# A fused two-block transformer kernel: which expert rows TensorE adds up, and when the second memory is fetched and normed

## The chip, the cores and the metric

One core of one Trainium2 chip runs the whole program. The metric is the device time in microseconds of one execution; lower is better. TensorE is called PE here (PEld is its weight load), VectorE DVE, ScalarE ACT, GpSimd POOL and SyncE SP.

## What is computed

The reference is two transformer blocks over 512 tokens of width 1024, all in fp32. The first block has a mixer (a gated short convolution and causal differential attention), cross-attention to a memory of 256 rows, and then the part that the change is about, a lookup of single-neuron experts:

```python
q = (hc @ w_pq).reshape(PEER_CHUNK, PEER_HEADS, 2, PEER_DK_HALF)
sc = jnp.einsum('thcd,chnd->thcn', q, sub_keys)
vals, idx = lax.top_k(sc, PEER_TOPK)              # per head and key half: 16 of 128
... # the 16x16 sums of both halves, top 16 of them -> experts, gates g (softmax)
ue = peer_u[experts]; ve = peer_v[experts]        # 16384 experts, rows of 1024
act = jax.nn.gelu(jnp.einsum('td,thkd->thk', hc, ue), approximate=False)
y = jnp.einsum('thk,thkd->td', g * act, ve)
```

Each token uses 8 heads x 16 = 128 experts. The second block has sparse attention, a gMLP and a convolution branch, cross-attention to a second memory (`mem_2`, normed with its own gain, then projected to keys and values), and a feed-forward of width 2816 with a short convolution.

## The kernel before

**Halves and tiles.** The tokens are 4 tiles of 128, and two tiles make a half. Half 0 goes through the first block's mixer and cross-attention alone. Then three streams run side by side until about 2390 us: `work` (the mixer of half 1, its cross-attention, its expert scores, the second memory, and the whole second block of half 0), `peers` (the experts of tiles 0 to 3) and `choices` (top-k selection of tiles 0 to 3). After that the second block of half 1 runs alone.

**What sets the order.** The class `Plan` is a host-side generator. `weave` gives each of the three streams a clock, always takes a step from the stream whose clock is lowest, and adds the number that the step carries. The result is one list of steps, and each engine executes, in that order, those of its instructions that belong to each step. All queues are in order, so an instruction that waits holds all behind it on its engine. Semaphores do the rest.

**One expert.** An expert number k = 128 t + c is column c of tile t: one of 128 experts for each of the tile's 128 tokens. POOL gathers its rows (U and V side by side, 128 x 2048 fp32, 1 MB) with an indirect DMA into one of 8 slots (L2073). DVE takes the dot product with the tokens (L1856, and writes over the U half). ACT applies the gelu (L1357) and multiplies by the gate (L1361, or L1364). Then the V row is added, in one of two ways:

- DVE: `scalar_tensor_tensor` into the residual tile X (L1836), one expert later in the order.
- PE: ACT first writes a diagonal matrix of the gates (L1369, tile DG or a piece of BIG), and PE multiplies it with the V row's two halves into PSUM banks 6 and 7 (L1092, L1093), placed two experts later in the order. At a tile's end DVE adds the two banks to X (L1846).

The slot is free for the gather of k+8 once the sum is done, so POOL waits for L1836 or L1093. `pe_sums` lists the experts that PE sums. Before, an expert is put there while `light` is set (in half 1's attention, cross-attention and expert scores, the second memory, and half 0's sparse attention), two of three.

**Choices.** `choose` finds the experts of one tile in 4 parts p of 2 heads each, on DVE: L1764, L1767 and L1772 (top 8 values, their places, and their removal), L1779, L1798, L1801, L1804, then L1811 writes the indices. Tiles 0 and 1 are chosen while tile 0's experts run (k = 0 to 74); that ends with part (1, 3). `work` may not load the weights of k (half 1's attention keys) before it, and their eviction to SBUF waits for it too.

**Projections.** Weights come in entries of 512 KB through a ring of 6 (SP queue, L698). A `proj_T` entry is 8 matmuls of 128x256 (L833 seven times, L834), a `proj_tok` entry L853 and L854. Each result takes one of 6 PSUM banks in turn while experts run. Sites are named by their weights: cc, cx, cb (convolution; DVE multiplies, L1565, L1570, L1582), cv, gc (DVE, L1587), q, k, v, then the attention `da`.

**Norms.** `norm_steps` is a norm's squares on ACT (L1139), mean and reciprocal on DVE (L1509, L1511), the root on ACT (L1144), and the product with the inverse root for both tiles, tile 1 on DVE (L1521), tile 0 on ACT (L1161) or, where `norm_of` says `pool=True`, on POOL (L2042). `trans` follows: 16 PE transposes (L821, L822) and the evictions with the gain (L1170 on ACT).

**The second memory.** `memory(2, True)` comes after all four quarters of the scores of half 1: ACT issues the load of `mem_2` (1 MB, L1129), waits, norms it, PE transposes it and projects it (sites nk, nv).

## Time and profile before

| | us |
|---|---|
| median of 3 runs | 3008.01 (3006.35 to 3032.95) |
| the profiled execution | 3006.38 |
| its span in the trace | 3004.7 |
| PE busy, share of the span | 2483.7 (83%) |
| DVE busy | 1812.6 (60%) |
| ACT busy | 1117.7 (37%) |
| mean granted PE clock | 0.887 |
| experts' gathers | 512, from 559.4 to 2364.6 us, 536.90 MB |

The span is what the profiler saw from the first to the last instruction; the execution's own time has 1.7 us around it, and the median of the runs is 1.6 us above the profiled one. Busy shares are means over stretches with different limits, so they say little by themselves: the three streams run from 559 to 2390 us, and within that each stretch has its own busiest engine. An expert's time is read by its dot product: k = 0 at 565.9 us, 74 at about 879, 93 at 926.5, 151 at 1101.4, 215 at 1331.0, 255 at 1524.8 and 511 at 2384.2.

### The profile page before, as it was taken

How to read it: one execution, taken by the hardware profiler on the slowest of the kernel's cores; microseconds unless marked ns; L12 is line 12 of the kernel's file. 1: busy time of each engine (PE TensorE's matmuls, PEld its weight loads, DVE VectorE, ACT ScalarE, POOL GpSimd, SP SyncE). 2: the span in 40 equal slices, each digit the busy share in tenths (PEclk: the TensorE clock that was granted, in tenths of full speed). 3: DMA queues.
4: the chain of work that ended last, by engine and by line, in shares of the span. 5: the costliest groups of instructions: out<-in, count | busy, mean ns of one | idle time of the engine just before them, and what ended most of it. 6: DMA issues, size and time to landing. Idle time of an engine off the chain costs nothing.

```text
span 3004.7 us, 29173 instructions
## 1 busy us (share of the span) xinstructions
PE 2483.7 (83%) x9938; PEld 1784.8 (59%) x9938; DVE 1812.6 (60%) x4267; ACT 1117.7 (37%) x2717; POOL 696.8 (23%) x568
## 2 busy tenths in 40 slices
PE   8999998776957779789768888588988399788998
PEld 7786765665843446547536744365863177655883
DVE  2101312699998678668779997778997705512430
ACT  1101312231525663543342576564552213512210
POOL 0000000122345344332223535344323301100100
PEclk9999999888978889899889578799999695799999
DMA  6545243779999999998689998899999740032443
GB/s 198 170 153 167 92 160 108 290 295 343 387 409 420 350 383 415 419 378 318 257 307 400 419 341 338 323 409 416 417 417 418 320 135 29 1 106 82 151 152 119
DMA packets 156644, 827.08 MB, mean 275 GB/s; under 512 B 16920, under 2 KB 20392, under 8 KB 90704
## 3 DMA queue, kind: packets, MB, share of 16 engines
q0 software_dynamic: 73728, 536.90, 44.7%
q1 hardware_dynamic: 78144, 276.21, 26.2%
q10 hardware_dynamic: 4624, 12.11, 1.1%
q8 instruction: 79, 1.29, 0.2%
q14 instruction: 69, 0.57, 0.1%
HBM read 816.74 MB, written 8.41 MB: 275 GB/s over the span
## 4 chain that ended last, share of the span: by engine, by line
PE 50%; DVE 22%; ACT 14%; DMA 9%; issue 4%; POOL 1%; ACTq 0%; DVEq 0%; SPq 0%
PE ps L833 21%; DVE X L1836 6%; DMA BIG<-in_uv,BIG 6%; DVE BIG L1856 6%; PE ps L853 5%; PE ps L854 5%; PE ps L834 3%; PE ps L1070 3%; ACT L1357 2%; PE ps L974 2%; DVE BIG L1767 1%; PE ps L1092 1%; ACT WK L1139 1%; PE ps L1093 1%; DMA BIG<-head_scratch 1%
## 5 line engine op out<-in xcount | busy, mean ns | idle before, releaser
L2073 POOL DMA_INDIRECT BIG<-in_uv,BIG x512 | 647.3, 1264 | 1706.9 <-DVE X L1836 693.9
L833 PE MATMUL ps<-BIG,RING 128*128 128x256 f32 x3472 | 812.6, 387 | 75.0 <-ACT BIG L1190 31.6
L833 PEld LDWEIGHTS ps<-BIG,RING 128*128 128x128 f32 x3472 | 671.6, 194 | 186.0 <-ACT BIG L1190 32.0
L1856 DVE CUSTOM_DVE_ANT_0 BIG<-BIG 128x1024 f32<-128x1024 f32 x512 | 620.2, 1217 | 54.2 <-DMA BIG<-in_uv,BIG 53.3
L1836 DVE SCALAR_TENSOR_TENSOR X<-BIG,small,X 128x1024 f32<-128x1024 f32 x378 | 484.2, 1281 | 86.6 <-ACT small L1361 86.4
L1357 ACT ACTIVATE small<-small 128x1 f32<-128x1 f32 x512 | 102.7, 201 | 703.6 <-DVE small L1856 702.0
L833 PE MATMUL ps<-WK,RING 128*128 128x256 f32 x1232 | 290.2, 388 | 16.1 <-DVE BIG L1615 14.2
L833 PEld LDWEIGHTS ps<-WK,RING 128*128 128x128 f32 x1232 | 238.0, 194 | 56.7 <-DVE BIG L1615 21.2
L853 PE MATMUL ps<-RING,BIG 128*128 128x512 f32 (+1 forms) x448 | 224.1, 582 | 7.1 <-DVE BIG L1594 4.4
L854 PE MATMUL ps<-RING,BIG 128*128 128x512 f32 (+1 forms) x448 | 223.5, 580 | 0.0
L1190 ACT ACTIVATE BIG<-ps 128x256 f32<-128x256 f32 (+2 forms) x143 | 56.3, 396 | 381.5 <-PE ps L834 322.8
L821 PE MATMUL ps<-ident,BIG 128*128 128x128 f32 x128 | 50.9, 404 | 150.0 <-ACT BIG L1161 83.1
L1553 DVE TENSOR_SCALAR BIG<-ps 128x256 f32<-128x256 f32 (+2 forms) x37 | 16.8, 454 | 255.8 <-PE ps L834 211.3
L1070 PE MATMUL ps<-RING,BIG 128*128 128x512 f32 x352 | 156.7, 607 | 8.9 <-DVE BIG L1615 8.9
L1357 ACT ACT_TABLE_LOAD x121 | 155.2, 1283 | 2.8 <-issue 0.6
L834 PE MATMUL ps<-BIG,RING 128*128 128x256 f32 x496 | 147.5, 379 | 0.0
L853 PEld LDWEIGHTS ps<-RING,BIG 128*128 128x128 f32 x448 | 84.9, 191 | 104.7 <-issue 92.2
L854 PEld LDWEIGHTS ps<-RING,BIG 128*128 128x128 f32 x448 | 85.4, 191 | 101.5 <-issue 100.1
L1546 DVE TENSOR_TENSOR X<-ps,X 128x512 f32<-128x512 f32 x40 | 27.3, 690 | 196.1 <-PE ps L854 124.8
L1139 ACT ACTIVATE WK<-X 128x1024 f32<-128x1024 f32 x32 | 33.8, 1056 | 258.2 <-DVE X L1546 242.7
L1070 PEld LDWEIGHTS ps<-RING,BIG 128*128 128x128 f32 x352 | 67.9, 194 | 96.8 <-issue 84.0
L821 PEld LDWEIGHTS ps<-ident,BIG 128*128 128x128 f32 x128 | 27.3, 213 | 159.4 <-ACT BIG L1161 88.0
(257 smaller groups left out, 3261.2 us busy)
## 6 DMA issues: line engine op xcount, KB each, us to landing
RING<-in_w_up SPq DMA_DIRECT2D x88, 512.0 KB, 6.1
RING<-in_w_down SPq DMA_DIRECT2D x44, 512.0 KB, 6.1
RING<-in_w_pq SPq DMA_DIRECT2D x32, 512.0 KB, 4.3
RING<-in_w_cc SPq DMA_DIRECT2D x16, 512.0 KB, 7.9
RING<-in_w_cx SPq DMA_DIRECT2D x16, 512.0 KB, 4.8
RING<-in_w_cb SPq DMA_DIRECT2D x16, 512.0 KB, 5.3
RING<-in_w_cv SPq DMA_DIRECT2D x16, 512.0 KB, 4.5
RING<-in_w_gc SPq DMA_DIRECT2D x16, 512.0 KB, 6.5
```

Source lines behind the costliest of these rows:

```text
L821: e.transpose(ps[:, 0:128], tmp[:, 0, k * 128:(k + 1) * 128], ident[:, :])
L833: e.matmul(ps[:, 0:256], W[:, j, :], src[:, j, 0:256], start=j == 0, stop=False)
L834: e.matmul(ps[:, 0:256], W[:, 7, :], src[:, 7, 0:256], start=False, stop=True).then_inc(pe.sem, pe("mm", site, h, c, m))
L853: e.matmul(ps[:, 0:n], src[:, 2 * j, t * 128:(t + 1) * 128], W[:, 0, :], start=j == 0, stop=False)
L854: mm = e.matmul(ps[:, 0:n], src[:, 2 * j + 1, t * 128:(t + 1) * 128], W[:, 1, :], start=False, stop=j == 3)
L974: mm = e.matmul(ps[pr, 0:nn], W1[l // 16][:, l % 16, :], KN[pr, s, f0:f0 + 16 * nn - 15:16], start=l == 0, stop=l == 31)
L1070: mm = e.matmul(ps[:, :], AF[:, f, t * 128:(t + 1) * 128], W[:, hh * 512:(hh + 1) * 512], start=f == 0, stop=f == 21)
L1139: e.activation(SQ[:, 0:width], src(i), ACT.Square, accum_out=small[:, o + i:o + i + 1]).then_inc(act.sem, act("sq", key, i))
L1357: e.activation(a, dots[:, k % 8:k % 8 + 1], ACT.Gelu).then_inc(act.sem, act("gelu", k))
L1836: e.scalar_tensor_tensor(out=X[:, t, :], in0=slot[slot_of[k]][:, 1024:2048], scalar=acts[:, k % 8:k % 8 + 1], in1=X[:, t, :], op0=ALU.mult ...
L1856: e.tensor_tensor_reduce(out=u, in0=HF[:, t % 2, :], in1=u, scale=1.0, scalar=0.0, op0=ALU.mult, op1=ALU.add, accum_out=dots[:, k % 8:k % ...
L2073: e.indirect_dma_start(out=slot[i], out_offset=None, in_=I["uv"], in_offset=bass.IndirectOffsetOnAxis(ap=IDX[:, t, c:c + 1], axis=0)).then ...
```

## The change

Four things change.

1. While part (1, 3) isn't chosen yet, an expert goes to PE every second time, although `light` is not set. These are 37 of the experts 0 to 74, which all were DVE's before.
2. A flag `norming` is set from a lean norm's start to the end of its transposes, and for the last two steps of half 1's and of half 0's attention units before one; while it is set, no expert goes to PE. Together with the shifted count this gives, by the plan, 59, 48, 37 and 17 experts on PE in tiles 0 to 3 (161), where it was 23, 54, 41 and 16 (134).
3. The load of `mem_2` is issued at the start of half 1's expert norm. Its norm comes after the second quarter of half 1's scores, the transposes after the fourth. For that its tile lies at W0 + 6144, where the values of the first block's cross-attention lay, which are dead by then.
4. The two norms of half 1's second block that used POOL for tile 0 use ACT.

```diff
@@ norm_steps, norm, da
     def norm_steps(self, key, lean):
         gap = 2.6 if lean else 0
+        self.norming = lean
         yield gap, "norm_sq", key
...
         for k in range(8):
             yield (cost if k == 7 else 0), "trans", key, k, lean
+        self.norming = False
...
-        yield from self.phase(True, (((5.0 if h == 0 else 9.0), "da", h, i) for i in range(20)))
+        for step in self.phase(True, (((5.0 if h == 0 else 9.0), "da", h, i) for i in range(20))):
+            self.norming = h == 1 and step[3] >= 18
+            yield step
@@ memory
-    def memory(self, tag, lean):
-        yield 0, "mark", ("mem", tag)
-        yield 0, "mem_in", tag
-        yield from self.norm(("mem", tag), lean)
-        yield from self.proj_T("mk" if tag == 1 else "nk", tag, 2, lean)
-        yield from self.proj_tok("mv" if tag == 1 else "nv", tag, 2, lean)
+    def memory(self):
+        yield from self.proj_T("nk", 2, 2, True)
+        yield from self.proj_tok("nv", 2, 2, True)
@@ experts
         yield 0, "mark", ("ffn", h)
+        if h == 1:
+            yield 0, "mem_in", 2
         yield from self.norm(("ffn", h), lean)
@@ scores
             for t in range(2):
                 yield 0.9, "scores", h, c, t, lean
+            if h == 1 and c == 1:
+                yield 0, "mark", ("mem", 2)
+                yield from self.norm_steps(("mem", 2), lean)
+                self.norming = False
+            if h == 1 and c == 3:
+                for i in range(8):
+                    yield 0, "trans", ("mem", 2), i, lean
@@ second (the 20 steps of the sparse attention; set back after the transposes of y)
-        yield from self.phase(True, ((8.0, "nsa", h, i) for i in range(20)))
+        for step in self.phase(True, ((8.0, "nsa", h, i) for i in range(20))):
+            self.norming = lean and step[3] >= 18
+            yield step
@@ peers
-                if self.light:
+                if not self.norming and (self.light or (1, 3) not in self.chosen):
                     n += 1
-                    if n % 3:
+                    if n % 3 if self.light else n % 2:
                         self.pe_sums[t].append(k)
@@ program, norm_of
-               2: dict(M=at_(W0 + 8192, 2, 1024), MT=at_(W0 + 10240, 8, 256), TMP=at_(W0 + 8192, 2, 1024),
+               2: dict(M=at_(W0 + 6144, 2, 1024), MT=at_(W0 + 10240, 8, 256), TMP=at_(W0 + 6144, 2, 1024),
...
-                return dict(src=half(h), g="mix2", dst=HTz, tmp=TMPz, o=0, pool=h == 1)
+                return dict(src=half(h), g="mix2", dst=HTz, tmp=TMPz, o=0, pool=False)
...
-                return dict(src=half(h), g="ffn2", dst=HTu, tmp=at_(L0, 2, 1024), o=0, pool=h == 1)
+                return dict(src=half(h), g="ffn2", dst=HTu, tmp=at_(L0, 2, 1024), o=0, pool=False)
```

The new lines shift the line numbers of the changed kernel by up to 15: L1092 and L1093 are L1107 and L1108 there, L833 is L848, L1139 is L1154, and so on.

How PE's queue changes while tiles 0 and 1 are chosen: the start of half 1's projections, at site cc, after the norm's transposes. The banks are ps0 to ps7. Before:

```order
L833 MATMUL ps5<-BIG,RING 128x256 x7
L834 MATMUL ps5<-BIG,RING 128x256
L833 MATMUL ps0<-BIG,RING 128x256 x7
L834 MATMUL ps0<-BIG,RING 128x256
L833 MATMUL ps1<-BIG,RING 128x256 x7
L834 MATMUL ps1<-BIG,RING 128x256
L833 MATMUL ps2<-BIG,RING 128x256 x7
L834 MATMUL ps2<-BIG,RING 128x256
```

The same place now:

```order
L848 MATMUL ps5<-BIG,RING 128x256 x7
L849 MATMUL ps5<-BIG,RING 128x256
L848 MATMUL ps0<-BIG,RING 128x256 x7
L849 MATMUL ps0<-BIG,RING 128x256
L1107 MATMUL ps6<-BIG,DG 128x512
L1108 MATMUL ps7<-BIG,DG 128x512
L848 MATMUL ps1<-BIG,RING 128x256 x7
L849 MATMUL ps1<-BIG,RING 128x256
L848 MATMUL ps2<-BIG,RING 128x256 x7
L849 MATMUL ps2<-BIG,RING 128x256
```

Between every second pair of weight entries stands a sum, two matmuls of 128x512 that need an expert's diagonal.

ACT's queue where the second memory is normed. Before, at the end of half 1's scores, right before PE's transposes of it (L1345 evicts the last scores):

```order
L1369 ACTIVATE BIG<-ident,small 128x128
L1129 DMA BIG<-in_mem_2 128x2x1024
L1139 ACTIVATE WK,small<-BIG 128x1024 x2
L1351 ACT_TABLE_LOAD
L1351 ACTIVATE BIG<-BIG 128x32
L1144 ACT_TABLE_LOAD
L1144 ACTIVATE small<-small 128x2
L1357 ACT_TABLE_LOAD
L1357 ACTIVATE small<-small 128x1
L1361 ACTIVATE small<-small,BIG 128x1
L1161 ACTIVATE BIG<-BIG,small 128x1024
```

Now, in the middle of the scores, with the load issued 62 rows earlier, ahead of the squares of the expert norm:

```order
L1384 ACTIVATE BIG<-ident,small 128x128
L1154 ACTIVATE WK,small<-BIG 128x1024 x2
L1372 ACTIVATE small<-small 128x1
L1376 ACTIVATE small<-small,BIG 128x1
L1159 ACT_TABLE_LOAD
L1159 ACTIVATE small<-small 128x2
L1176 ACTIVATE BIG<-BIG,small 128x1024
L1372 ACT_TABLE_LOAD
```

The load no longer stands right ahead of the squares that need it. The evictions of the third quarter (L1205) now stand behind the norm in this queue.

PE's queue at the end of half 1's attention, from the last of the 16 transposes (ps4) into the projection ga. Before:

```order
L821 MATMUL ps4<-ident,BIG 128x128
L822 MATMUL ps4<-ident,BIG 128x128
L833 MATMUL ps5<-BIG,RING 128x256 x7
L834 MATMUL ps5<-BIG,RING 128x256
L1092 MATMUL ps6<-BIG 128x512
L1093 MATMUL ps7<-BIG 128x512
L833 MATMUL ps0<-BIG,RING 128x256 x7
```

The sum there is expert 151's, and POOL's gather for its slot waits for it. Now:

```order
L836 MATMUL ps4<-ident,BIG 128x128
L837 MATMUL ps4<-ident,BIG 128x128
L848 MATMUL ps5<-BIG,RING 128x256 x7
L849 MATMUL ps5<-BIG,RING 128x256
L848 MATMUL ps0<-BIG,RING 128x256 x7
L849 MATMUL ps0<-BIG,RING 128x256
```

The sum behind the first entry of ga is gone, and so are the last ones ahead of the transposes: the experts 145, 146, 148, 149 and 151 are DVE's.

## Rows read from the trace of the kernel before

**Rows 1.** The page's groups: line, engine, operation, count, busy us, mean ns

```profile
L1856 DVE CUSTOM_DVE_ANT_0 BIG<-BIG 128x1024 f32<-128x1024 f32 x512 | 620.2, 1217 | 54.2 <-DMA BIG<-in_uv,BIG 53.3
...
L1836 DVE SCALAR_TENSOR_TENSOR X<-BIG,small,X 128x1024 f32<-128x1024 f32 x378 | 484.2, 1281 | 86.6 <-ACT small L1361 86.4
```

**Rows 2.** Waits, whole span: us in total, times, longest us

```profile
POOL BIG L2073 <- DVE X L1836: 693.9, 303, 9.6
...
POOL BIG L2073 <- PE ps L1093: 418.1, 99, 28.8
```

**Rows 3.** Windows: busy PE, PEld, DVE, ACT, POOL, PEclk, DMA share, GB/s

```profile
565.90:870.00 304.10, 227.37 (x1017) 197.19 (x1015) 284.25 (x707) 100.83 (x244) 79.87 (x73) 0.88 0.93 361
...
722.00:752.00 30.00, 7.99 (x35) 6.40 (x35) 29.93 (x78) 3.98 (x16) 8.13 (x9) 0.72 0.92 345
...
786.00:848.00 62.00, 62.00 (x289) 54.59 (x288) 56.14 (x128) 34.62 (x65) 17.46 (x15) 1.00 1.02 417
...
848.00:882.00 34.00, 9.26 (x43) 7.80 (x42) 33.73 (x67) 6.14 (x21) 13.00 (x11) 0.70 1.02 419
...
882.00:930.00 48.00, 36.22 (x96) 19.29 (x96) 46.16 (x61) 15.19 (x53) 30.57 (x20) 0.89 1.00 406
```

**Rows 4.** Waits of PE from 566 to 930 us

```profile
PE ps L833 <- ACT BIG L1190: 31.6, 1, 31.6
...
PE ps L833 <- DVE BIG L1582: 22.0, 2, 21.1
...
PE ps L821 <- DVE BIG L1521: 17.7, 1, 17.7
...
PE ps L950 <- ACT BIG L1190: 16.7, 2, 14.4
```

**Rows 5.** Chain of waits, 1433 to 1536 us: start, us, what

```profile
1433.23 10.63 DMA BIG<-in_mem
...
1456.61 3.26 PE ps L833 x14
...
1460.30 0.86 PE ps L1092 x2
...
1461.16 0.86 PE ps L1093 x2
...
1535.12 0.87 PE ps L1093 x2
```

**Rows 6.** Line L1369: count, min/median/max ns

```profile
L1369 ACT ACTIVATE DG<-ident,small x68: 401/402/403, 930.8 to 2384.9; 128x128 f32<-128x128 f32 x68
```

**Rows 7.** Timeline of PE at 751 us: start, us, instruction, count

```profile
751.32 5.36 PE L833 MATMUL ps<-BIG,RING 128*128 128x256 f32 x14 [21.12 <-DVE BIG L1582]
...
756.95 3.19 PE L833 MATMUL ps<-BIG,RING 128*128 128x256 f32 x14
```

**Rows 8.** Waits of PE and of DVE from 1336 to 1545 us

```profile
PE ps L821 <- ACT BIG L1161: 29.3, 2, 20.8
...
DVE small L1509 <- ACT WK L1139: 13.4, 1, 13.4
```

**Rows 9.** Windows around the second memory's norm

```profile
1384.00:1432.00 48.00, 44.89 (x188) 33.96 (x186) 43.74 (x149) 16.39 (x43) 11.54 (x12) 0.96 0.85 308
...
1432.00:1453.00 21.00, 0.80 (x4) 0.80 (x5) 7.45 (x35) 9.09 (x16) 1.45 (x1) 0.57 0.45 171
```

**Rows 10.** Waits of POOL from 1095 to 1130 us

```profile
POOL BIG L2073 <- PE ps L1093: 19.4, 3, 17.1
```

**Rows 11.** Windows at two norms, at 1113 and at 1900 us

```profile
1113.00:1125.00 12.00, 12.00 (x50) 10.07 (x49) 11.90 (x20) 5.72 (x10) 2.17 (x3) 0.82 0.56 203
...
1900.00:1912.00 12.00, 2.67 (x13) 2.71 (x14) 6.70 (x17) 8.09 (x24) 1.15 (x2) 0.50 0.26 87
```

**Rows 12.** Timeline: POOL at half 1's last norm; an ACT copy alike

```profile
2758.20 3.40 POOL L2042 TENSOR_SCALAR BIG<-X,small 128x1024 f32<-128x1024 f32 x1 [157.96 <-ACT small L1144]
...
1451.02 1.13 ACT L1161 ACTIVATE BIG<-BIG,small 128x1024 f32<-128x1024 f32 x1
```

More of the change, by code:

```diff
@@ L232, in mixer @@
             yield (3.0 if k == 7 else 0), "trans", ("o", h), k, lean
+        self.norming = False
         yield from self.proj_T("ga", h, 2, lean)
@@ L280, in scores @@
                 yield 0.9, "scores", h, c, t, lean
+            if h == 1 and c == 1:
+                yield 0, "mark", ("mem", 2)
+                yield from self.norm_steps(("mem", 2), lean)
+                self.norming = False
+            if h == 1 and c == 3:
+                for i in range(8):
+                    yield 0, "trans", ("mem", 2), i, lean
             self.reached.add(("sc", h, c))
@@ L330, in second @@
             yield (2.0 if k == 7 else 0), "trans", ("y", h), k, lean
+        self.norming = False
         yield from self.proj_tok("ou", h, 2, lean)
@@ L368, in work @@
             yield step
-        for step in self.memory(2, True):
+        for step in self.memory():
             self.light = True
@@ L1287, in mem_in @@
                     for q in ENGINES:
-                        w.wait_ge(*at["mark", ("mem", tag), q])
+                        w.wait_ge(*at["mark", ("ffn", 1), q])
                 load(f"mem{tag}", m["M"], I[m["src"]].rearrange("a (t p) d -> p (a t) d", p=128), "mem", tag)
```

## The prediction

> **What bounds the kernel now.** I read the page's groups first, to see what an expert costs and who adds it: the dot product takes 1217 ns of DVE, and 378 of 512 sums are DVE's at 1281 ns [rows 1]. So a DVE sum doubles an expert's price there. Then the waits, to see who holds the slots: POOL waited 693.9 us for DVE's sums and 418.1 us for PE's [rows 2], 2.3 us a sum (303) against 4.2 us (99). Then the windows, stretch by stretch, because each has its own limit.
>
> While tiles 0 and 1 are chosen (565.9 to about 880 us, experts 0 to 74), DVE is busy 284.25 of the first 304.1 us, the DMA moves 361 GB/s where saturated stretches show 417 to 419, and PE is busy 227.37 us [rows 3]. DVE is the fullest. But within the stretch the limits change places: from 722 to 752 us DVE has 29.93 of 30 us and PE 7.99; from 786 to 848 us PE is busy all 62 us and the DMA is full; from 848 to 882 us DVE has 33.73 of 34 us and PE 9.26 [rows 3]. PE's four longest waits there are 31.6 us (the eviction of the keys, held until part (1, 3) is chosen), 21.1 of 22.0 us (cb waits for DVE's L1582), 17.7 us (the norm) and 14.4 of 16.7 us [rows 4]; this is the room for sums on PE.
>
> From 1336 us, after half 1's expert norm, the chain of waits runs through PE: from 1456.61 to the last sum of tile 1, which starts at 1535.12, entries and sums follow each other without a hole. The one large hole ahead of them is the second memory's norm, which begins with its load, 10.63 us [rows 5]. PE waits 20.8 us for ACT's product with the root there, DVE 13.4 us for the squares [rows 8], and from 1432 to 1453 us PE is busy 0.80 us and the DMA runs at 0.45 [rows 9].
>
> **Part 1, every second sum on PE until (1, 3) is chosen.** 37 sums leave DVE: 37 x 1.281 = 47.4 us less of 284.25 plus what runs to 880 us. They come to PE, and one is two pieces of 0.86 us in an unbroken chain [rows 5], 1.72 us: 37 x 1.72 = 63.6 us more. ACT writes 37 diagonals of 402 ns [rows 6], 14.9 us on an engine that is busy 100.83 of 304.1 us [rows 3]; nothing for that, since its idle time hides it (15 us at most if that cover were gone).
>
> Upper bounds of the gain: the DMA must move 361 x 304.1 GB/s x us, at 417 that is 263 us, so 41 us at most; DVE, 47 us at most. The tighter one is PE. Over 565.9 to 930 us (with the keys' and values' entries behind the choices) it is busy about 227 + 4 + 36 = 267 us, the 4 being its share of 870 to 882 us. With the sums it has 331 us of 364. Some idle time must stay: the norm's own chain, waits for the first multiplications, the start behind the choices; I take 10 to 35 us. That gives 341 to 366 us, a gain of 23 to -2 us.
>
> The pieces in order: the norm ends earlier by the five sums that DVE no longer makes ahead of it, 6 us. PE then reaches cb later by ten sums, 17 us, which mostly uses up the 21.1 us wait, while DVE comes there some 19 us earlier; start of cb some 8 to 10 us earlier. From 752 to 848 us PE has no idle time, and 12 more sums cost it 21 us, so it ends q about 12 us later than now; but behind q it waits 31.6 us today, so this is covered. DVE's choices, ten experts further, need 33.73 us now and five sums less, 27 us, and can run up to the slots' depth ahead of PE; (1, 3) would be chosen some 15 us earlier. What is late next are PE's entries for keys and values: today five of them already stand in PSUM when (1, 3) comes, and now sums of experts up to 72 stand ahead of them in PE's queue, so perhaps two do. Three entries of some 3.5 us each (14 of their 16 passes take 3.19 to 3.26 us) [rows 5, 7], 10 us, are then missing, and the DMA is full from 882 to 930 us as well (406 GB/s) [rows 3]. I take 12 us, the middle of the bound from PE's sum, with both ends kept (23 and -2), and -10 as the end where chances of order fall badly.
>
> Of the clock, the trace shows that the first 14 matmuls after the 21.1 us wait took 5.36 us and the next 14 took 3.19 [rows 7], which is 1.2 against 2.4 GHz for part of them; the mean granted clock is 0.72 in that window and 1.00 from 786 us. The Trainium skill (TensorE: Matmul & The Clock Gate, "Why this matters for your kernels") says to leave no idle gaps between bursts, because the clock drops after them. By that rule sums that fill the gaps pay back some 2 us at each of three gaps, and the gain would be 18 instead of 12 us; the trace agrees that there is a loss behind a gap, but the gaps become shorter rather than disappear.
>
> **Part 2, the memory.** The load goes out about 110 us before it is needed, at a time when ACT waits for all engines anyway (the marks of the expert norm), so its wait of 10.63 us goes. The norm's steps then run while PE works on the scores. The wait of PE, 20.8 us, goes whole, since only the 16 transposes stay. Is something else late in its place? DVE is busy 43.74 of 48 us from 1384 to 1432 us [rows 9], but only 7.45 of the next 21 us, so its choice work fits if it flows over. The norm now stands in ACT's queue ahead of evictions of pq, and ACT waits for DVE's reciprocal; PE runs up to six banks ahead, 20 us, so I charge 1 to 5 us and take 3. The plan puts two sums less on PE in this stretch (27 for 29), 3 us less; the last two parts of tile 3's choices slip by one or two experts into DVE's full stretch behind, about 1 us. Sum 20.8 - 3 + 3 - 1 = 20 us, range 12 to 24. Floor: nothing if PE's hole just moves.
>
> **Part 3, no sums beside a norm.** At the end of half 1's attention POOL waits 17.1 us for one PE sum that stands behind 16 transposes and an entry [rows 10], and the DMA falls to 203 GB/s for 12 us; before the second block's norm in half 0 it falls to 87 GB/s for 12 us [rows 11]. With DVE as the adder, slots free earlier: of these holes of 6 and 9.5 us I count 4 us in all, since the DVE chain that causes the norm itself stays, and DVE gets up to two sums, 2.6 us, ahead of each norm. Range -4 to 10. Tiles 1 and 2 have 10 sums more on DVE, 13 us in stretches where DVE isn't full: nothing.
>
> **Part 4, POOL to ACT.** Twice POOL takes 3.40 us for a product on which the transposes wait, where ACT takes 1.13 us for such a copy [rows 12]: 2 x 2.27 = 4.5 us off a chain with nothing beside it. The Trainium skill (GPSIMD Engine Reference, "4.1 Engine selection") calls one-input elementwise work on GpSimd "roughly line-rate", by which the move would bring next to nothing and the sum below would be 4.5 us smaller; the row disagrees, and the measured 3.40 us decides.
>
> **The sum.** 12 + 20 + 4 + 4.5 = 40.5 us off the span of 3004.7 is 2964; with the 1.7 us around the span and the 1.6 us between the profiled execution and the median it is 2968 us, 1.3% faster. Without a change of kernel, a measurement here can tell about 1% apart.
>
> **Rivals.**
> - *PE takes over as the bound while tiles 0 and 1 are chosen.* For it: PE is at 100% for 62 us at a stretch [rows 3], and each sum adds 1.72 us there. Against it: the 31.6 us wait behind. Part 1 then gives -5 instead of 12: 2985 us.
> - *The relief goes through whole.* PE's idle time shrinks to 10 us, and the DMA holes at the norms close: part 1 gives 23, part 3 gives 10: 2951 us. Against it: the DMA is saturated from 786 us on.
> - *The memory's norm only moves its hole.* If ACT, waiting for DVE's reciprocal, holds the evictions past the six banks, PE stands still in the scores. Part 2 gives 5: 2983 us.
> - *Slower.* PE's queue holds the slots. A PE sum kept POOL waiting 4.2 us against 2.3 us for DVE's [rows 2]; if that reaches the gathers, 37 x 1.9 = 70 us are lost, with nothing of the 47 us gained, and 3008 + 70 - 28.5 (parts 2 to 4) = 3050 us. It decides once DVE's dot products wait for gathers over the whole stretch; today that wait is 53.3 us over the whole program [rows 1].
>
> That the change doesn't do what it says is no rival: the instruction order shows it.
>
> **Chances.** Forecast 0.46 (own range 2955 to 2981), PE as bound 0.23, relief whole 0.14, the hole moved 0.10, slower 0.07. Faster by over 1% means below 2978: most of the forecast (0.39), the whole relief (0.14) and some of the two that lie between (0.08), 0.61. Slower by over 1% is 0.06, the rest, 0.33, is within 1%. The range from 2944 to 3001 leaves out the slower rival and the tails of the others.
>
> **What would show it.** Right: 161 PE sums; experts 0 to 74 in about 300 us instead of 313, with DVE near 80% and PE near 90% in it; no PE wait of 20 us near 1440, and tile 1's last sum about 32 us earlier than 1535; DMA above 300 GB/s in the 12 us behind half 1's attention norm; no POOL product in the last 600 us. Wrong: DVE waiting for gathers from 600 to 850 us, PE waiting for L1369's diagonals (then the sums come too early in its queue), or a new PE wait of over 10 us within the scores. The largest unknown is how much of DVE's 47 us survives PE's 64.

## The result, and the profile after

The changed kernel takes 2983.74 us (median of 18 runs, 2974.98 to 3003.74) against 3007.79 us before in the same measurement (18 runs, 3003.32 to 3038.33): a ratio of 0.9904 with an interval of 0.9876 to 0.9931, 1.0% faster. The ratio takes in all runs; that of the two medians is 0.9920, since six of the 18 runs before took 3027 us or more. The forecast was 2968 us and 1.3%. The profiled execution has a span of 2990.2 us and a mean granted clock of 0.897, against 3004.7 us and 0.887. It took 2992.0 us, 8.3 us more than the median, so that the trace shows less of the gain than the runs do.

The page's groups for the dot products and DVE's sums, of after:

```profile
L1871 DVE CUSTOM_DVE_ANT_0 BIG<-BIG 128x1024 f32<-128x1024 f32 x512 | 618.9, 1219 | 64.6 <-DMA BIG<-in_uv,BIG 63.1
L1851 DVE SCALAR_TENSOR_TENSOR X<-BIG,small,X 128x1024 f32<-128x1024 f32 x351 | 450.3, 1283 | 103.7 <-ACT small L1376 103.5
```

351 sums are DVE's where 378 were [rows 1], so PE has 161. The lines quoted here have numbers 15 higher than before (L1856 is now L1871). In two windows, the choices of tiles 0 and 1 (dots 0 to 74) and the stretch to dot 93, with PE, PEld, DVE, ACT and POOL busy, clock, DMA share and GB/s:

```profile
563.80:864.20 300.40, 265.62 (x1067) 202.77 (x1067) 250.85 (x685) 115.52 (x284) 88.86 (x75) 0.95 0.95 362
864.20:921.60 57.40, 57.40 (x196) 37.79 (x195) 45.33 (x64) 16.93 (x54) 24.25 (x19) 0.98 1.02 418
```

The first took 313.1 us and takes 300.4; PE is now 88% busy in it and DVE 84%. The second took 47.5 us and takes 57.4, and PE has not one idle moment in it; before it was busy 36.22 of about 48 us [rows 3]. Of 12.7 us won, 9.9 are given back. PE's waits in the first window show what the sums filled; 31.6 and 21.1 us were the longest before [rows 4]:

```profile
PE ps L836 <- DVE BIG L1536: 13.3, 1, 13.3
PE ps L965 <- ACT BIG L1205: 8.8, 1, 8.8
PE ps L1107 <- ACT DG L1384: 6.0, 3, 3.3
PE ps L1107 <- ACT BIG L1384: 5.6, 3, 4.0
```

At the second memory PE's waits from 1330 to 1540 us are now these, where 20.8 us stood for the norm [rows 8]:

```profile
PE ps L836 <- ACT BIG L1176: 8.4, 1, 8.4
PE ps L965 <- ACT BIG L1205: 8.0, 2, 7.4
PE ps L1107 <- ACT BIG L1384: 6.2, 1, 6.2
PE ps L848 <- ACT BIG L1185: 2.9, 2, 1.9
PE ps L1107 <- ACT DG L1384: 2.3, 1, 2.3
PE ps L836 <- ACT BIG L1185: 1.3, 1, 1.3
```

The 8.4 us are the expert norm's own, which was there before. The scores' longest wait for an eviction is 7.4 us; it was 2.5 us. Behind half 1's attention POOL waits (1085 to 1125 us) for DVE's sum where it waited 17.1 us for PE's [rows 10], and at the second block's norm (1876 us) the DMA is as empty as it was [rows 11]:

```profile
POOL BIG L2088 <- DVE X L1851: 20.8, 10, 13.7
POOL BIG L2088 <- PE ps L1108: 1.0, 1, 1.0
```

```profile
1876.00:1888.00 12.00, 3.27 (x16) 3.06 (x16) 6.42 (x17) 8.13 (x24) 2.17 (x2) 0.54 0.26 87
```

In half 1's norms ACT and DVE make a tile each at the same time, 1.15 us, instead of 3.40 us on POOL [rows 12]:

```profile
2373.61 1.15 ACT L1176 ACTIVATE WK<-X,small 128x1024 f32<-128x1024 f32 x1
2373.61 0.75 DVE L1536 TENSOR_SCALAR WK<-X,small 128x1024 f32<-128x1024 f32 x1 [0.27 <-ACT small L1159]
```

Set against the first dot of each trace, the gain is then 12.7 us at dot 74, 2.8 at 93, 2.7 at 213, 16.9 at the mix2 norm's transposes in half 0 (1002.0 and 985.1 us behind the first dot), 22.0 at dot 363 and 24.0 at the last. Behind that 11.5 us are lost. The place is half 1's sparse attention, from the end of the compression's matmuls to the first transpose of the y norm: 136.2 us before, 154.7 now. I call it **the late stretch**. Windows of 30 us in it, before and after; PEclk is the column ahead of the DMA share:

```profile
2484.00:2514.00 30.00, 27.44 (x167) 23.02 (x166) 15.32 (x76) 11.10 (x29) 3.84 (x3) 0.50 0.18 69
2514.00:2544.00 30.00, 30.00 (x103) 23.73 (x102) 19.36 (x96) 14.43 (x48) 5.12 (x4) 0.50 0.00 1
2544.00:2574.00 30.00, 30.00 (x99) 21.88 (x99) 16.10 (x77) 11.77 (x33) 6.08 (x4) 0.54 0.00 1
2574.00:2604.00 30.00, 30.00 (x208) 24.87 (x206) 21.82 (x107) 21.28 (x55) 8.00 (x5) 1.00 0.01 2
```

```profile
2458.00:2488.00 30.00, 26.59 (x134) 21.00 (x133) 19.57 (x97) 14.34 (x40) 5.12 (x4) 0.56 0.11 36
2488.00:2518.00 30.00, 30.00 (x105) 23.99 (x104) 16.63 (x85) 12.17 (x40) 5.12 (x4) 0.50 0.00 1
2518.00:2548.00 30.00, 30.00 (x95) 21.64 (x94) 16.51 (x77) 12.19 (x33) 4.79 (x3) 0.50 0.00 1
2548.00:2578.00 30.00, 30.00 (x101) 22.74 (x100) 14.15 (x68) 11.16 (x31) 4.79 (x3) 0.50 0.00 1
2578.00:2608.00 30.00, 22.33 (x147) 19.95 (x145) 14.58 (x64) 13.09 (x32) 3.20 (x2) 0.78 0.00 1
```

The work is the same. PE does it at 1.2 GHz (0.50), about 100 matmuls in 30 us, until the clock is granted in full, then 208. The next lines narrow down its return, to some 2571 us of the span before and to 2580 us now:

```profile
2566.00:2574.00 8.00, 8.00 (x32) 6.00 (x31) 5.10 (x23) 3.73 (x10) 1.60 (x1) 0.66 0.00 0
```

```profile
2575.00:2583.00 8.00, 8.00 (x35) 6.14 (x34) 4.19 (x21) 3.73 (x10) 1.60 (x1) 0.69 0.00 0
```

The stretch begins at 2495.3 and at 2464.6 us, so the clock is back 76 us into it before and 115 us into it now. These 39 us more of PE's work at half the clock are worth about half as much, and the stretch is 18.5 us longer.

### The profile page after: what moved, and what is told of

It reads as the page before. It is cut to its first block, busy times and chain, and to the rows that moved or that the text cites. A ratio compares the mean times of both kernels' runs of the same rounds, so it can differ in the third digit from the quotient of the medians.

```text
span 2990.2 us, 29389 instructions
## 1 busy us (share of the span) xinstructions
PE 2533.2 (85%) x10046; PEld 1804.9 (60%) x10046; DVE 1781.5 (60%) x4240; ACT 1130.7 (38%) x2747; POOL 706.2 (24%) x566
## 4 chain that ended last, share of the span: by engine, by line
PE 56%; DVE 18%; ACT 12%; DMA 9%; issue 4%; POOL 1%; ACTq 0%; DVEq 0%; SPq 0%
PE ps L848 25%; DMA BIG<-in_uv,BIG 7%; PE ps L868 6%; PE ps L869 5%; DVE BIG L1871 5%; DVE X L1851 4%; PE ps L849 3%; PE ps L1085 3%; ACT L1372 2%; PE ps L989 2%; PE ps L1107 2%; PE ps L1108 2%; PE ps L1057 2%; DMA BIG<-head_scratch 1%; PE ps L1036 1%
## 5 line engine op out<-in xcount | busy, mean ns | idle before, releaser
L2088 POOL DMA_INDIRECT BIG<-in_uv,BIG x512 | 663.6, 1296 | 1664.5 <-DVE X L1851 575.4
L848 PE MATMUL ps<-BIG,RING 128*128 128x256 f32 x3472 | 804.1, 384 | 15.9 <-DMA RING<-in_w_cq 4.8
L848 PEld LDWEIGHTS ps<-BIG,RING 128*128 128x128 f32 x3472 | 667.7, 193 | 134.5 <-issue 26.7
L1871 DVE CUSTOM_DVE_ANT_0 BIG<-BIG 128x1024 f32<-128x1024 f32 x512 | 618.9, 1219 | 64.6 <-DMA BIG<-in_uv,BIG 63.1
L1851 DVE SCALAR_TENSOR_TENSOR X<-BIG,small,X 128x1024 f32<-128x1024 f32 x351 | 450.3, 1283 | 103.7 <-ACT small L1376 103.5
L848 PE MATMUL ps<-WK,RING 128*128 128x256 f32 x1232 | 287.3, 385 | 18.7 <-DVE BIG L1630 16.7
L848 PEld LDWEIGHTS ps<-WK,RING 128*128 128x128 f32 x1232 | 235.9, 193 | 58.8 <-DVE BIG L1630 23.9
L1205 ACT ACTIVATE BIG<-ps 128x256 f32<-128x256 f32 (+2 forms) x143 | 56.4, 397 | 398.0 <-PE ps L849 338.3
L1107 PE MATMUL ps<-BIG,DG 128*128 128x512 f32 x162 | 97.2, 685 | 56.8 <-ACT DG L1384 56.7
L1154 ACT ACTIVATE WK<-X 128x1024 f32<-128x1024 f32 x32 | 33.8, 1056 | 257.5 <-DVE X L1561 243.4
```

The source lines that it names most:

```text
L848: e.matmul(ps[:, 0:256], W[:, j, :], src[:, j, 0:256], start=j == 0, stop=False)
L1107: e.matmul(banks[6][:, :], d, v[:, 0:512], start=first, stop=last)
L1851: e.scalar_tensor_tensor(out=X[:, t, :], in0=slot[slot_of[k]][:, 1024:2048], scalar=acts[:, k % 8:k % 8 + 1], in1=X[:, t, :], op0=ALU.mult ...
L1871: e.tensor_tensor_reduce(out=u, in0=HF[:, t % 2, :], in1=u, scale=1.0, scalar=0.0, op0=ALU.mult, op1=ALU.add, accum_out=dots[:, k % 8:k % ...
L2088: e.indirect_dma_start(out=slot[i], out_offset=None, in_=I["uv"], in_offset=bass.IndirectOffsetOnAxis(ap=IDX[:, t, c:c + 1], axis=0)).then ...
```

## Experiments

Three theories were open at the start: that part 1's gain is lost at the keys' and values' entries; that the memory's norm, ahead of the evictions in ACT's queue, makes the new 7.4 us wait; and that part 4, which alone touches what lies directly ahead of the late stretch, keeps its clock low. Against each stands that the difference is the scatter between executions. Twelve kernels were run, the changed one again among them. Each ratio is against runs of the kernel before made together with it. Their medians were 3011.3 us for the four single parts, 3016.7 for pool_norms, mix2_pool, early_keys and split_norm, 3009.9 for the extra matmuls and all_sums, and 3006.6 for the changed kernel again, so medians of different measurements don't rank kernels by themselves.

**One part at a time.** Each is the kernel before with one part of the change:

```diff
 # sums_only: part 1, without the norming flag
+                if self.light or (1, 3) not in self.chosen:
+                    if n % 3 if self.light else n % 2:
 # memory_only: part 2 (mem_in in experts, norm_steps and transposes in scores, the new addresses)
 # norms_only: part 3, on the old sums
+                if self.light and not self.norming:
 # act_norms_only: part 4
-    mix2, ffn2: pool=h == 1
+    mix2, ffn2: pool=False
```

> The kernel before with part 1 alone (every second sum on PE until (1, 3) is chosen). Theory A (PE takes the gain back right behind the choices): experts 0 to 74 take some 300 us instead of 313, experts 74 to 93 some 57 instead of 47.5 us, so 3 us are left at expert 93; PE has an unbroken run of about 58 us through the keys' and values' entries. Theory B (the loss there comes from something else in the full change): experts 74 to 93 stay at 48 us and 12 us are left at expert 93. Total, by A: within 6 us of before; by B 12 us faster.

> The kernel before with part 2 alone (memory loaded at the expert norm, normed among the scores). Theory A (a new wait inside the scores eats a third): PE waits some 7 us for an eviction of pq that stands behind the norm in ACT's queue, and the stretch from the expert norm's transposes to those of the second block's norm (499.8 us from 502.2 before) becomes 13 to 14 us shorter. Theory B (the smaller gain comes from the sums that were shifted): no such wait, 20 us shorter.

> The kernel before with part 3 alone (no sum on PE beside a norm). Theory A (it is worth next to nothing, since the DVE chain of the norm sets the time): total within 4 us of before, POOL's 17.1 us wait at 1105 us gone. Theory B: slots that come free earlier fill the DMA hole, 4 to 8 us faster, and most of it behind half 1's attention and half 0's sparse attention.

> The kernel before with part 4 alone (two products from POOL to ACT). Everything up to the last expert is the same program, so up to there nothing moves. Behind it: 2.3 us less at each of the two norms, 4.5 us in all. What the sparse attention of half 1 between them takes (136 us before, 155 us in the changed kernel, with PE's granted clock at half for longer) tells the theories apart on that loss: if it is caused by part 4 it shows here too in the profile and in the times (about 14 us slower); if it is a matter of chance of the clock, it takes 136 us here or 155 us, whatever the kernel.

| kernel | median us (runs) | ratio, interval | profiled span | late stretch | span less its excess over 136.2 |
|---|---|---|---|---|---|
| before | | | 3004.7 | 136.2 | 3004.7 |
| changed | 2983.7 (18) | 0.9904, 0.9876 to 0.9931 | 2990.2 | 154.7 | 2971.7 |
| sums_only | 3020.5 (10) | 1.0018, 0.9988 to 1.0048 | 3020.9 | 162.4 | 2994.7 |
| memory_only | 3003.6 (10) | 0.9966, 0.9925 to 1.0006 | 3005.8 | 150.1 | 2991.9 |
| norms_only | 2999.3 (10) | 0.9947, 0.9912 to 0.9982 | 3031.0 | 168.2 | 2999.0 |
| act_norms_only | 3024.0 (10) | 1.0027, 0.9999 to 1.0055 | 3016.1 | 154.7 | 2997.6 |

By their ratios the four parts bring -0.2, 0.3, 0.5 and -0.3%, 0.4% together, while the whole brings 1.0%. The last column seems to agree better: 10.0, 12.8, 5.7 and 7.1 us, 35.6 together, and 33.0 for the whole. How good this is depends on scatter: a second execution of the changed kernel (below) gives 25.5, and all four differences lean on the one trace before. That the late stretch spoils the sum of the ratios is likely by this, not shown. Part 4 alone makes the two norms shorter and yet measured no faster.

Part 1 alone, its two windows:

```profile
564.00:867.40 303.40, 267.90 (x1069) 203.61 (x1068) 249.77 (x684) 115.80 (x285) 85.89 (x75) 0.94 0.93 359
867.40:924.30 56.90, 56.90 (x195) 37.53 (x194) 45.24 (x64) 16.90 (x54) 25.52 (x19) 0.98 1.02 419
```

9.7 us are won to dot 74 and 9.4 given back by dot 93 (360.2 us in all, 360.6 before). Part 2 alone: from the expert norm's to the mix2 norm's transposes 218.7 us instead of 231.9, 13.2 us less. Part 3 alone: the POOL wait at 1100 us is DVE's, 13.6 us, and row 213 comes 2.6 us earlier.

**The control on scatter.** The program of act_norms_only is the kernel before's up to the last row, and still its dot 151 came 4.0 us later and dot 303 3.4 us. Then the changed kernel was run again:

> The changed kernel itself, unedited, on the chip of this call. Theory E (the moment at which TensorE's clock returns in half 1's sparse attention differs between executions, and its spread is the spread of the times): up to the last row's dot this execution agrees with the first one within 5 us (1789 to 1799 us behind the first dot), the stretch from the compression's end to the y transposes is again anywhere from 136 to 168 us, the profiled span less what the stretch takes above 136.2 us is 2967 to 2977 us, and the runs lie between 2972 and 3010 us. Rival F (the moment is a property of the kernel, and the edits of the other experiments moved it): the stretch is 150 to 158 us again, and the median 2980 to 2988 us.

2985.1 us (12 runs, 2978.7 to 3013.0), ratio 0.9917 (0.9881 to 0.9954). The two executions agree within 1.3 us up to dot 363, 1855 us into the span, and differ by 6.8 us at the last dot. Four more traces below are of the same program up to the last dot; all six lie within 1.5 us of each other at dots 93 and 120, but spread over 6 us at dots 213 and 363 and over 7.7 us at the last. So behind dot 120 a single trace tells an effect below some 6 to 8 us from scatter only where it shows the wait. The late stretch took 154.8 us, against 154.7; rival F's number, where theory E left 136 to 168 open, and the median is in F's range as well. The span less the excess is 2979.2, above the 2967 to 2977 that E wanted. These two profiles don't show the scatter of the runs to be the late stretch's.

**Part 4 undone in the changed kernel**, for both norms and for mix2 alone:

```diff
-            if kind == "mix2":  ... pool=False)
+            if kind == "mix2":  ... pool=h == 1)
-            if kind == "ffn2":  ... pool=False)     # pool_norms only
+            if kind == "ffn2":  ... pool=h == 1)    # pool_norms only
```

> The changed kernel with part 4 undone: GpSimd again makes the squares and the scaling of the norms before half 1's two last expert layers. The two norms themselves should take their 4.5 us back (last dot to the mix2 transposes 18.8 instead of 16.7 us, x(2,1) to ffn2's transposes 91 instead of 88.8). Theory A: ACT's norm is what keeps TensorE at 1.2 GHz longer in half 1's sparse attention (154.7 us from the end of the compression to the y transposes instead of 136.2). Then this stretch is 136 to 142 us again and the time is 2965 to 2975 us, ratio 0.985 to 0.989. Rival B: when the clock returns there is chance or hangs on everything before it. Then the stretch is anything between 136 and 168 us, and the median is that of the changed kernel plus 4.5 us, 2986 to 2990 us, ratio 0.991 to 0.993.

> The changed kernel with part 4 undone for the mix2 norm alone, the one ahead of the stretch at 1.2 GHz; ffn2's norm, behind the stretch, stays on ACT. Theory A (ACT's mix2 norm keeps the clock low longer): stretch 136 to 142 us, time 2962 to 2973 us, ratio 0.984 to 0.988, and 2.3 us below the kernel with both norms on GpSimd. Rival B (chance): 2985 to 2988 us, ratio 0.991 to 0.993.

Only the products move; the squares are ACT's in every kernel, though the expectation gives them to GpSimd. Medians 3009.7 us (12 runs, ratio 0.9947, 0.9914 to 0.9980) and 3006.5 us (12, 0.9947, 0.9914 to 0.9981). The late stretch took 162.4 and 150.0 us. Theory A falls: with POOL back in its place the stretch is not short again. Both are above rival B's medians too. The spans less the excess are 2978.4 and 2978.0 us.

**More work for PE in the late stretch.** If the clock's return hung on how much PE does there, extra matmuls would bring it earlier. The score matmuls are issued twice, into the same PSUM:

```diff
+                        if h and j == 0 and u < 8:    # more_cols_32: if h and j < 2
+                            e.matmul(ps[:, 0:nn], q, K, start=True, stop=True)
                         e.matmul(ps[:, 0:nn], q, K, start=True, stop=True).then_inc(...)
```

> The changed kernel, with the first score matmul of the first 8 of 16 units of half 1's sparse attention issued twice (same operands, same PSUM, the second overwrites the first), in the stretch that runs at 1.2 GHz: 8 matmuls of 384 columns, some 7 us more if the clock stays low. Theory C (how much TensorE has to do in this stretch decides when its clock returns, and the changed kernel is near the edge): the clock is back at 185 us behind the last dot or sooner, the stretch from the compression's end to the y transposes is 120 to 142 us in place of 154.7, and the runs lie close together, 2968 to 2985 us. Rival D (TensorE's load there does not matter to it): the stretch is 143 to 175 us as by chance, and the median is 2988 to 2993 us.

> As the kernel with 8 matmuls doubled, but with both large score matmuls of all 16 units of half 1's sparse attention issued twice: 32 more, of 384 and 512 columns, some 30 us more at 1.2 GHz and 15 at 2.4. Theory C: the clock is back in the first 60 us of the stretch, which then takes 110 to 135 us, and the time is 2955 to 2980 us. Rival D (the load does not matter): the stretch is 165 to 200 us, and the median 3005 to 3015 us.

3006.1 us (10 runs, 2982.8 to 3017.7; ratio 0.9980, 0.9952 to 1.0009), stretch 144.0 us; and 3032.8 us (10, 3011.5 to 3057.2; 3025.2 without the longest, which the ratio leaves out; 1.0089, 1.0053 to 1.0126), stretch 173.2 us. The first stretch alone could be read either way (theory C wanted 120 to 142, rival D 143 to 175), but its runs are scattered over 35 us. The clock is back 84 us into it with 8 more matmuls and 105 us with 32, where the changed kernel has 115 us and the kernel before 76. Both lie within what kernels without extra work show, the larger load has the later return, and neither is near the first 60 us, where theory C had it for 32. In that form theory C falls; a small effect of the load within this scatter isn't excluded. Less its excess, extra matmuls included, the spans are 2976.3 and 2972.8 us: the same program everywhere else.

**The keys ahead again.** No PE sum from row 63 on while tile 1 is chosen:

```diff
-                if not self.norming and (self.light or (1, 3) not in self.chosen):
+                if not self.norming and (self.light or ((1, 3) not in self.chosen and k < 63)):
```

> The changed kernel, but with no sum on TensorE from row 63 on while tile 1 is chosen, so that key and value entries can run ahead again (row 74 then comes about 3 us later than in the changed kernel). Theory (TensorE had 58 us of unbroken work there, 864 to 922 us, and its key entries came late): the dot of row 93, counted from the first dot, comes 9 to 12 us before that of the kernel before instead of 2.8, and the time is 4 to 8 us below the changed kernel's 2984, ratio 0.988. Rival (the gain is lost to whatever comes next, since DVE has its sums back): row 93 moves by less than 3 us, 2984 us, ratio 0.9905.

```profile
563.00:868.20 305.20, 273.15 (x1141) 215.62 (x1139) 256.65 (x689) 113.84 (x281) 88.66 (x75) 0.96 0.94 362
868.20:920.80 52.60, 36.73 (x96) 19.64 (x96) 46.37 (x64) 15.38 (x51) 28.39 (x19) 0.86 1.01 420
```

The entries do run ahead: PE has 15.9 us free in the second window. But DVE, with its sums back, is 4.7 us later at dot 74, and dot 93 comes at 357.7 us behind the first, against 357.8 in the changed kernel: the rival's reading, for this step. What the second window shows is a full DMA, 420 GB/s; it is 418 in the changed kernel's, 419 in sums_only's and 406 from 882 to 930 us before [rows 3]. The gathers of rows 74 to 93 are at the DMA's limit either way. Dot 120 came 6.3 us earlier than in the changed kernel, where the traces of that program differ by 1.5 us at most, so this is real; but by dot 151 it was 2.3 us later, and the gain was gone. The time was 2979.2 us (6 runs, 2974.5 to 2984.0), ratio 0.9872 (0.9835 to 0.9908), the lowest of all, but its late stretch took 136.2 us, and less the excess its span of 2978.8 us is not below the changed kernel's 2971.7 and 2979.2. Its intervals overlap with the changed kernel's as well. It isn't shown to be better.

**The memory's norm in two pieces**, root and product a quarter later:

```diff
             if h == 1 and c == 1:
-                yield from self.norm_steps(("mem", 2), lean)
+                yield 0, "norm_sq", ("mem", 2); yield 0, "norm_inv", ("mem", 2)
+            if h == 1 and c == 2:
+                yield 0, "norm_root", ("mem", 2); yield 0, "norm_out", ("mem", 2)
```

> The changed kernel with the second memory's norm in two pieces: squares and their sum after the second quarter of the key scores, root and scaling after the third. Theory (the scores' evictions wait behind the whole norm in ACT's queue, 7.4 us at 1409.6): TensorE's longest wait of its score matmuls on an eviction falls below 4 us, the stretch from ffn(1)'s to mix2(0)'s transposes shrinks from 217.8 to about 213 us, and the time is 3 to 5 us lower, 2980 us, ratio 0.989. Rival (the second piece makes its own wait, and the memory's transposes come later): the two add up to the same 217 to 219 us, 2984 us, ratio 0.9905.

Its waits of PE from 1380 to 1460 us:

```profile
PE ps L968 <- ACT BIG L1208: 8.2, 2, 7.3
PE ps L839 <- ACT BIG L1188: 4.1, 1, 4.1
```

The wait of the scores for the eviction is 7.3 us as before, and a wait of the memory's transposes for their evictions comes in addition; from transposes to transposes the stretch takes 222.7 us against 217.8. The time was 3010.4 us (12 runs, ratio 0.9967, 0.9940 to 0.9995), its late stretch 168.2 us.

Going by the wait alone would clear the norm, but the wait misleads. The starts of the second and the third quarter's scores, first in the kernel before and then in split_norm, are

```profile
1380.12 1.95 PE L950 MATMUL ps<-WK,BIG 128*128 128x128 f32 x16
1403.53 3.23 PE L950 MATMUL ps<-WK,BIG 128*128 128x128 f32 x16 [2.49 <-ACT BIG L1190]
```

```profile
1374.45 1.95 PE L968 MATMUL ps<-WK,BIG 128*128 128x128 f32 x16
1402.68 3.75 PE L968 MATMUL ps<-WK,BIG 128*128 128x128 f32 x16 [7.32 <-ACT BIG L1208]
```

That is 23.4 us before and 28.2 with the norm's first piece alone in this quarter. With the whole norm, in the changed kernel, it is 34.3 us (34.0 in memory_only, 22.6 in sums_only and norms_only, which don't have it). So the norm in this place costs some 11 us; PE has one sum more there than before, which its 7.4 us wait covers. Its second piece moved away gives 6.1 of them back, and 1.7 us are lost in the next quarter and 9.2 from the last scores to the transposes behind. The first eviction of the third quarter shows it: it starts 7.7 us after the second scores before (1387.77), 12.6 in split_norm and 14.4 in the changed kernel. What follows it, PE and ACT around the wait in the changed kernel, is

```profile
1373.49 1.95 PE L965 MATMUL ps<-WK,BIG 128*128 128x128 f32 x16
1399.32 1.02 PE L1108 MATMUL ps<-BIG,DG 128*128 128x512 f32 x2
1407.78 3.75 PE L965 MATMUL ps<-WK,BIG 128*128 128x128 f32 x16 [7.44 <-ACT BIG L1205]
```

```profile
1400.61 0.20 ACT L1372 ACTIVATE small<-small 128x1 f32<-128x1 f32 x1 [4.78 <-DVE small L1871]
1400.84 0.29 ACT L1379 ACTIVATE small<-small,BIG 128x1 f32<-128x1 f32 x1
1401.17 0.40 ACT L1384 ACTIVATE BIG<-ident,small 128x128 f32<-128x128 f32 x1
1401.48 0.36 ACT L1205 ACTIVATE BIG<-ps 128x256 f32<-128x256 f32 x1
1406.84 0.20 ACT L1372 ACTIVATE small<-small 128x1 f32<-128x1 f32 x1 [5.00 <-DVE small L1871]
1407.07 0.29 ACT L1376 ACTIVATE small<-small,BIG 128x1 f32<-128x1 f32 x1
1407.27 0.36 ACT L1205 ACTIVATE BIG<-ps 128x256 f32<-128x256 f32 x1
```

In ACT's queue one row's activation and one eviction take turns. The activation waits 4.78 and 5.00 us for its dot product, since DVE, busy 23.01 of 24 us from 1386 to 1410, works on tile 2's choices between two dots. The eviction behind it was ready, and PE waited for it. The kernel before has the same turns, with waits of 4.45 and 5.29 us, but its evictions had begun earlier and took 15.3 us from the first to the fourth, where they take 19.4 now. So 6.8 of the 11 us are the norm's delay of the first eviction, and the rest are longer turns behind it.

**All sums of that phase on PE**, the rival in which it becomes the bound:

```diff
-                    if n % 3 if self.light else n % 2:
+                    if n % 3 if self.light else True:
```

> The changed kernel, but every V row's sum is TensorE's while tiles 0 and 1 are chosen, 37 or so more than in the changed kernel. Theory (TensorE becomes the bound, as the rival of the prediction has it): a sum there is four matmuls of 0.55 us, so 37 more are 80 us on an engine that is busy 268 of 303 us; the stretch from the first dot to that of row 74 grows from 300 to 345 us or more, and the time to 3020 to 3035 us. Rival (DVE is still what the slots wait for, and TensorE's waits swallow the sums): the stretch stays at 300 to 310 us, 2985 to 2995 us.

```profile
564.50:901.50 337.00, 321.29 (x1207) 228.66 (x1205) 210.57 (x650) 129.00 (x321) 82.20 (x77) 0.98 0.88 319
```

```profile
POOL BIG L2088 <- PE ps L1108: 235.1, 68, 14.9
```

3029.5 us (10 runs), ratio 1.0069 (1.0037 to 1.0101), as expected. The window is 337.0 us, 36.6 more than with half of the sums, PE is busy 95% of it and POOL waits 235.1 us for its sums. The window is shorter than the 345 us that four matmuls of 0.55 us a sum gave; at half the sums PE had 35 us free, of which 16 remain.

## Why the prediction was right, and where not

**What bounds the stretches: right.** With every second sum on PE both engines stand at 88 and 84%, dots 0 to 74 take 300.4 us where "about 300" was written, and with all sums on PE it is the bound. The rival "PE takes over" begins beyond the change, between 37 and 74 sums.

**Part 1: 12 us forecast, 2.8 at dot 93 in the changed kernel and 0.4 alone.** The pieces were about right: (1, 3) was to be chosen some 15 us earlier and dots 0 to 74 to take about 300 us (12.7 us won), and the keys' and values' entries were to be late by 10 us (9.9 given back). They leave 5 us at most. The price of the sums was right as well: PE is busy 323.0 us to dot 93 and was busy 263.6, so 37 sums cost 59.4 us where 63.6 were forecast. The step that failed is the one behind them, "I take 12 us, the middle of the bound from PE's sum": that middle stands for some 22 us of PE idle to the end of the entries, out of the 10 to 35 that the text allowed, and the windows show 34.8, the far end, all of it ahead of dot 74, where the norm (13.3 us), the scores' first eviction (8.8) and PE's waits for diagonals (11.6 in six, one of the text's own signs of being wrong) stayed. The sum should have gone by the pieces. And early_keys adds what the text named only in passing: with the entries out of the way dots 74 to 93 can't be made up either, since the DMA is full there, by its 418 to 420 GB/s. In the span less the excess sums_only stands 10.0 us below before. That surplus arises behind dot 303, where no wait was found that part 1 removes; whether it is more than scatter stays open.

**Part 2: 20 us forecast, 13 to 14 measured** (13.2 alone, 14.1 in the changed kernel, transposes to transposes), inside 12 to 24. The hole of 20.8 us is gone as said. The term that was mis-sized is the charge for ACT's queue, 3 us: the quarter of the scores that now holds the norm takes 34.3 us instead of 23.4, 10.9 more. From the last scores to the transposes behind, 23.0 us are won (140.2 us before, 117.2 now), and what lies ahead and between adds 2 us. The reason was half right: the norm does delay the evictions, but no term had what then holds them, activations that wait for dots. The text's cover of six banks, 20 us, was not enough for both. The rival "the hole only moves" took the right queue and priced it 15 us above the forecast, where 8 came true. "Tile 1's last sum about 32 us earlier", a sign of being right, failed: L1108 starts it at 1519.05 us, L1093 did at 1534.95, 16 us.

**Part 3: 4 us forecast; 2.6 to 5.7 us, not distinguishable from scatter.** POOL's wait changed its releaser, 17.1 us for PE's sum against 13.7 for DVE's, and the DMA's hole at the second norm is unchanged at 87 GB/s. The text expected the DMA above 300 GB/s behind the attention; from 1102 to 1114 us it is 346, from 1108 to 1120 262. The second window is the place of the 203 GB/s before, measured from the transposes, so this sign failed. The measured ratio of norms_only, 0.9947, says more, but it carries the late stretch too.

**Part 4: 4.5 us forecast, 4.4 seen.** From the last dot to the mix2 transposes 16.7 us instead of 18.8, from cross attention's transposes to ffn2's 88.8 instead of 91.1. Here the row's 3.40 us, against 1.15 us now, decided rightly. By the rule of the Trainium skill (GPSIMD Engine Reference, "4.1 Engine selection": "roughly line-rate") nothing was to be won, and this trace disagrees.

**The sum.** 40.5 us were forecast. Less the late stretch's excess the two executions of the changed kernel are 33.0 and 25.5 us faster than before's. Of this 2.8 us are there at the expert norm (parts 1 and 3), 14.1 come with part 2 and 4.4 with part 4, 21.3 in all. Between the mix2 norm's transposes in half 0 and the last dot the first execution gains 7.1 us more and the second 0.6; no wait was found for it. The change of the late stretch, 18.5 us in the profiled execution, was in no step and no rival, and is the largest single difference in either direction; what it was in the median run isn't known. The range, 2944 to 3001, held the time because its upper end left room for part 1 and part 2 to fail. That this room also covered the late stretch, which nobody had thought of, was luck.

**The clock.** The prediction used it only for what sums gain by filling gaps (2 us at each of three, by the rule that it quotes). From 751.8 to 831 us PE is busy all the time at a granted 1.00. Of the four long waits ahead of dot 74 the two longest, 31.6 and 21.1 us, are gone, and the granted clock of that window is 0.95 where it was 0.88. The 4.2 us by which 37 sums were cheaper than forecast are the most that this can have given back there, against some 6 us by the rule in the forecast; no part of the gain is shown to be the clock's. In the late stretch, from 2488 to 2578 us, the records show PE without a gap at 0.50. The Trainium skill (TensorE: Matmul & The Clock Gate, "Why this matters for your kernels") says to leave no idle gaps; by these rows that is not enough to get the clock back.

**Open.** What decides when the clock returns in the late stretch. Fourteen profiles show 136.2 (twice), 140.7, 144.0, 150.0, 150.1, 154.7 (twice), 154.8, 162.4 (twice), 168.2 (twice) and 173.2 us, the last and 144.0 with extra matmuls. In the two with 168.2 us, norms_only and split_norm, the clock doesn't come back within the stretch at all. Neither the engine of the norm ahead of it nor, as far as two traces tell, more matmuls in it sets the value. That the runs' scatter (29 us in the changed kernel) comes from it is likely, not shown. Every run's mean granted clock is on record: of 102 runs of the kernel before, the 72 below 3022 us have 0.882 to 0.890 and the other 30, 3022 to 3039 us, 0.876 to 0.882, so the longer runs are those with less of PE's clock, though the record doesn't say where. The profiled runs with 168.2 us were the slowest of their 10 and 12. Rival F, that the kernel sets how long the stretch tends to be, isn't refuted either: 6 of 30 runs of the changed kernel took over 3000 us, 8 of 12 of mix2_pool, whose only difference is one norm's product, worth 2.3 us, and none of 6 of early_keys. The chips differed too, except between the last two.

## What to carry to other kernels

Count a gain at the first point where another resource is full, not at the end of the phase that is relieved: here 12.7 us at dot 74 were 2.8 us nineteen rows later. In a queue that serves two streams, an eviction costs what the instruction ahead of it waits for; look for the queue's wait, not for its busy time. Judge an edit by the time between two fixed points and not by the wait in it: with the norm split the wait stayed at 7.3 us, and the quarter became 6.1 us shorter. When parts are measured one at a time, set the same stretches of each trace side by side before adding ratios, and run the same program twice to see from what size on a difference counts.

## What the hardware did that I had not expected

PE at 1.2 GHz for 121 us with no idle time in its records, from 2512 to 2633 us of norms_only, of which the first 90 are:

```profile
2512.00:2542.00 30.00, 30.00 (x106) 24.26 (x106) 17.52 (x88) 12.80 (x41) 5.92 (x5) 0.50 0.00 1
2542.00:2572.00 30.00, 30.00 (x91) 20.99 (x90) 15.50 (x70) 11.57 (x32) 4.79 (x3) 0.50 0.00 1
2572.00:2602.00 30.00, 30.00 (x101) 22.74 (x100) 14.16 (x67) 11.19 (x30) 4.80 (x3) 0.50 0.00 0
```

The same matmuls in early_keys get the full clock from the second of these windows on:

```profile
2524.00:2554.00 30.00, 30.00 (x115) 22.10 (x113) 17.89 (x81) 13.60 (x39) 4.80 (x3) 0.60 0.00 1
2554.00:2584.00 30.00, 30.00 (x207) 25.02 (x206) 19.00 (x97) 18.65 (x49) 8.00 (x5) 1.00 0.00 1
```

The difference, 168.2 against 136.2 us for the same work, is larger than any part of the change brought. Their ends being modelled, matmul records that touch each other don't prove that PE was full.
